# The order of the matmuls in a GEMM chunk of a decoder layer: output tile by output tile, or k tile, product, output tile

## The reference

```python
h = rmsnorm(x, norm_mix)
parts = split(h @ w_in)                      # u, Bg, Cg, q/k/v of 3 head groups, g_a, g_b
A = (Bg * dwconv3(Cg * u)) @ w_conv_out      # short gated convolution
B = merged_attention(q, k, v) @ w_attn_out   # 3 dilated window groups; the samples read caches
x = x + (sigmoid(g_a) * A + sigmoid(g_b) * B) @ w_out
up, gate = split(rmsnorm(x, norm_ffn) @ w_ffn_in)
x = x + (silu(dwconv3(gate) + b) * up) @ w_ffn_down
y = rmsnorm(x, norm_final)
```

## Time and profile before

| | |
|---|---|
| median of 3 runs | 1557.56 us (1556.78 to 1562.81) |
| the profiled execution: span, first to last instruction | 1559.4 us |
| TensorE matmuls (PE) | busy 1527.8 us, 98%, 12354 matmuls |
| TensorE weight loads (PEld) | busy 1512.0 us, 97% |
| VectorE (DVE) | busy 895.9 us, 57% |
| ScalarE (ACT) | busy 693.6 us, 44% |
| GpSimd (POOL) | busy 75.8 us, 5% |
| mean granted TensorE clock | 0.993 |
| HBM | 210 GB/s over the span |

### The profile page before, as it was taken

How to read it: one execution, slowest core, us unless ns; L and a number is a source line. 1 busy time by engine, 2 the same in 40 slices (tenths; PEclk the granted TensorE clock), 3 DMA queues, 4 the chain that set the end, 5 groups by cost and what they waited for, 6 DMA issues and landing times.

```text
span 1559.4 us, 32031 instructions
## 1 busy us (share of the span) xinstructions
PE 1527.8 (98%) x12354; PEld 1512.0 (97%) x12354; DVE 895.9 (57%) x1057; ACT 693.6 (44%) x761; POOL 75.8 (5%) x145
## 2 busy tenths in 40 slices
PE   8999999999989999999999999989999999999997
PEld 8999999999988889999999999989999999999997
DVE  8646455756655434676665555664444656556554
ACT  7444444434444334444554444443333444444452
POOL 2000001002130000010000000000000000000000
PEclk9999999999999999999999999999999999999998
DMA  8867576557986636555577777775555666565552
GB/s 276 276 179 250 178 228 184 150 150 200 258 246 198 215 112 201 175 162 188 176 243 243 230 232 222 244 240 163 178 183 176 169 188 183 173 184 183 184 176 97
DMA packets 145141, 307.79 MB, mean 197 GB/s; under 512 B 10145, under 2 KB 10273, under 8 KB 144561
## 3 DMA queue, kind: packets, MB, share of 16 engines
q1 hardware_dynamic: 139120, 268.73, 56.2%
q0 software_dynamic: 5952, 38.12, 7.6%
HBM read 301.39 MB, written 26.38 MB: 210 GB/s over the span
## 4 chain that ended last, share of the span: by engine, by line
PE 96%; DVE 2%; issue 1%; ACT 0%; DMA 0%; SPq 0%; DVEq 0%; ACTq 0%
PE acc L919 31%; PE acc L920 31%; PE acc L921 31%; PE side L1058 1%; DVE w_lo L554 1%; PE side L1012 1%; PE side L991 1%; DMA raw<-w_in 0%; ACT w_hi L356 0%; DVE yg L900 0%; PE side L1003 0%; DVE tf L809 0%; PE side L978 0%; DVE tf L813 0%; DVE gate_a L731 0%
## 5 line engine op out<-in xcount | busy, mean ns | idle before, releaser
L554 DVE TENSOR_TENSOR w_lo<-raw,w_hi 128x1024 fp32r<-128x1024 f32 x503 | 617.2, 1236 | 546.5 <-ACT w_hi L356 544.4
L356 ACT ACTIVATE w_hi<-raw 128x1024 fp32r<-128x1024 f32 x503 | 530.0, 1059 | 742.1 <-PE acc L921 680.8
L919 PE MATMUL acc<-h_hi,w_hi 128*128 128x264 f32 x2872 | 821.5, 286 | 6.6 <-DVE gate_a L731 4.6
L921 PE MATMUL acc<-h_hi,w_lo 128*128 128x264 f32 x2872 | 817.5, 285 | 0.2 <-issue 0.2
L920 PE MATMUL acc<-h_lo,w_hi 128*128 128x264 f32 x2872 | 817.6, 285 | 0.0
L919 PEld LDWEIGHTS acc<-h_hi,w_hi 128*128 128x128 f32 x2872 | 542.8, 189 | 9.1 <-DVE gate_a L731 5.2
L920 PEld LDWEIGHTS acc<-h_lo,w_hi 128*128 128x128 f32 x2872 | 541.9, 189 | 0.1
L921 PEld LDWEIGHTS acc<-h_hi,w_lo 128*128 128x128 f32 x2872 | 540.7, 188 | 0.4 <-issue 0.4
L919 PE MATMUL acc<-f_hi,w_hi 128*128 128x264 f32 x704 | 201.1, 286 | 4.0 <-DVE f_lo L871 4.0
L921 PE MATMUL acc<-f_hi,w_lo 128*128 128x264 f32 x704 | 200.8, 285 | 1.2 <-issue 1.2
L920 PE MATMUL acc<-f_lo,w_hi 128*128 128x264 f32 x704 | 200.8, 285 | 0.0
(11 more groups left out here) (188 smaller groups left out, 851.6 us busy)
## 6 DMA issues: line engine op xcount, KB each, us to landing
raw<-w_in SPq DMA_DIRECT2D x183, 512.0 KB, 4.2
raw<-w_ffn_in SPq DMA_DIRECT2D x176, 512.0 KB, 4.1
raw<-w_ffn_down SPq DMA_DIRECT2D x88, 512.0 KB, 4.2
raw<-w_out SPq DMA_DIRECT2D x32, 512.0 KB, 4.5
s_kv<-cache POOLq DMA_DIRECT2D x16, 1020.0 KB, 9.1
raw<-w_conv_out SPq DMA_DIRECT2D x16, 512.0 KB, 4.6
raw<-w_attn_out SPq DMA_DIRECT2D x8, 512.0 KB, 4.7
s_kv<-cache POOLq DMA_DIRECT2D x8, 508.0 KB, 5.0
```

Of the source, the lines that this page charges most:

```text
L356: act.activation(w_hi[:, s % RING], raw[:, s % RING], ACT.Copy).then_inc(hi_ready, 1)
L554: dve.tensor_tensor(w_lo[:, s % RING], raw[:, s % RING], w_hi[:, s % RING].bitcast(F32), ALU.subtract).then_inc(lo_ready, 1)
L919: pe.matmul(out, w_hi[:, slot, k, cols], m_hi[:, kt + k, :], start=first and k == 0, stop=False)
L921: mm = pe.matmul(out, w_lo[:, slot, k, cols], m_hi[:, kt + k, :], start=False, stop=last and k == 1)
```

## The change

In every chunk that is not its group's last, the matmuls are written k tile by k tile, in it product by product, and in it output tile by output tile. Each matmul then writes another bank than the one before it. The waits on `psum_free` stand ahead of the first four matmuls of a group, one for each bank. A group's last chunk keeps its order, tile by tile, and its `tile_done`. `first_chunk` is not touched.

```diff
                 pe.wait_ge(lo_ready, 4 * quad + s + 1)
                 slot = s % RING
+                if not last:
+                    for k in range(2):
+                        for n, (w, x_k) in enumerate(((w_hi, m_hi), (w_hi, m_lo), (w_lo, m_hi))):
+                            for m in range(TILES):
+                                if first and k + n == 0:
+                                    pe.wait_ge(psum_free, TILES * group + m + 1)
+                                mm = pe.matmul(acc[:, m, 0:T], w[:, slot, k, m * P:(m + 1) * P], x_k[:, kt + k, :],
+                                               start=first and k + n == 0, stop=False)
+                    mm.then_inc(slots_free, 1)
+                    return
                 for m in range(TILES):
                     if first:
                         pe.wait_ge(psum_free, TILES * group + m + 1)
```

## The result

| | before | changed |
|---|---|---|
| median of 4 runs each | 1559.28 us | 1578.70 us (1578.05 to 1582.83) |
| ratio | | 1.0129, 95% interval 1.0110 to 1.0149 |
| profiled execution: time, span | span 1559.4 us | time 1579.13 us, span 1577.3 us |
| mean granted clock | 0.993 | 0.996 |

The change makes the kernel slower by 1.3%, 20 us (17 to 23). Forecast were 1583 us and a range of 1568 to 1600.

The account below looks back on a forecast made before the run. TensorE was taken to bound the kernel (96% of the chain). Pauses of 23.3 + 0.3 + 2.0 = 25.6 us on the 1559.4 us span gave 1585.0, stated as 1583 because the span lies 1.8 us above the median; range 1568 to 1600.

Parts of the forecast that it names:

- the ordinary and the partly covered boundaries: Between groups: 49 ordinary boundaries pause TensorE for 23.3 us in all; two partly covered ones cost 0.3 us.
- attn_out: Stage with late bank reads: new order loses 1.0 us at each of three boundaries, not in full; 2.0 us taken.
- (a): In 437 chunks, 10,488 steps on TensorE go to another bank than the one before; cost taken as 0.
- The spare 1 ns per step: Uncertainty of the steps that change bank: 1 ns either way not excluded, 10 us each way, kept for the range.
- (b): Group's first chunk: bank waits move to matmuls 1 to 4; TensorE pauses for last read's end + 0.05 − 0.25 us.
- the three types: Boundaries by reader of the banks: FFN type pauses 0.44 us, L818 type 0.56 us, ScalarE type 0.39 us.
- Restarting adds nothing: After a wait at a boundary, the held matmul runs 0.1 us behind its load, as undisturbed; no extra cost.
- The ring: In attn_out, t_hi, w_hi, w_lo and reads turn by themselves in 7.1 us without TensorE, so the loss can't add up fully.
- gate_a, 0: Four boundaries after gate_a groups: pauses disappear in the key-load loop, cost 0; uncovered, 0.5 to 1.0 us each.
- Faster and slower steps: Rivals on TensorE's step: 10 ns less, 105 us gained, 1478, chance 0.12; 3 ns more, +31 us, 1614, chance 0.08.
- Absorption: Rival: boundary pauses shrink TensorE's other waits, above all in gate_a; 10 to 15 us back, 1568 to 1573; chance 0.10.
- The falling clock: Rival: each boundary's pause drops TensorE to 1.2 GHz for one chunk; 132 us, 1715; chance 0.03.

Follow-up runs that it names:

- second measurement: The changed kernel once more, on one chip with the kernel before: 1577.21 us, ratio 1.0150 (1.0127 to 1.0172).
- the middle chunks alone: New order only in chunks neither first nor last in their group, against the kernel before: 1556.57 us against 1555.11, ratio 1.0010.
- the pairs: New order in middle chunks; in a group's first chunk banks 0 and 1 alternate, then 2 and 3; against the kernel before: 1555.47 us, ratio 0.9993.
- the split's place: VectorE's weight split moved to between bank reads 2 and 3: in the kernel before 1555.25 us, ratio 1.0000; in the changed kernel 1609.57 us, ratio 1.0347.
- the late split: The changed kernel with VectorE's weight split moved from between reads 0 and 1 to between reads 2 and 3: 1609.57 us, ratio 1.0347.
- the run with gate_a alone: New order only in the four gate_a groups, all their chunks but the last, against the kernel before: 1555.96 us against 1555.46, ratio 1.0005.
- the run with all chunks: The changed kernel with each group's last chunk in the new order too: 1712.01 us, ratio 1.1004 (1.0973 to 1.1034).

## Why the prediction was right

The direction, the mechanism and the size hold. Point by point:

- *The sum.* 25.6 us were forecast against 20 us (17 to 23) and, in the second measurement, 23 us (20 to 27) measured: the sum lies above the first interval and within the second. The pauses themselves came as summed: the ordinary and the partly covered boundaries, priced at 23.3 + 0.3 us, lost 23.5 and 23.6 in two profiles, attn_out 1.1 instead of 2.0. That makes 24.6 or 24.7. The two profiled spans differ by only 17.9 us; the kernel before lost about 5 us to its clock in gate_a and conv_out and 1.3 us to a wait in down_b in its execution. Why the medians of the first measurement lie 20 us apart and not 25 isn't shown. That the forecast of 1583 us lies only 4 us from the median is due in part to the kernel before, which ran 1.7 us above the 1557.56 that it started from.
- *(a), alternating steps, taken as 0.* Shown by the middle chunks alone (1.0010) and by the pairs (0.9993). That one step in six already turned to another bank in the old order, at no other pace, was enough evidence. The spare 1 ns per step wasn't needed: the step moved by less than 0.1 ns, about 1 us in all.
- *(b), the pause per boundary.* This is also where the rule of the Trainium skill on rotating banks ("Perfetto Trace Analysis", Matmuls) pointed, and the split's place shows it: with the waits apart a read of 1.4 us is overlapped, with the waits together it is paid. 0.44, 0.56 and 0.39 us predicted, 0.46, 0.56 and 0.39 measured in the three types. The rule used (end of the last read + 0.05 us − 0.25 us) also gave the 1.2 us of the late split and its 31 us in total, measured as 31 to 34.
- *Restarting adds nothing.* Held: after the late load at 940.62 the next starts at 940.73.
- *attn_out, 2.0 us (1.3 to 3.1).* Too large, though the reason given for absorption was right. The stage grew by 1.5 us (25.3 to 26.8), but 0.5 of that is the ordinary pause behind gate_b's last group. Its own boundaries lost 0.5, 0.6, 0.0 and, into w_out, 0.0 us, the same in both profiles of the changed kernel: 1.1 us. At the last two TensorE had already waited 1.2 us for the late reads in the old order, ahead of a first chunk's seventh matmul, and at the one before them 0.6 us; now it waits 1.2 us in all at each of the three, from the second matmul on (one of them before, then two changed):

```profile
666.22 0.39 PE L919 MATMUL acc<-att_hi,w_hi 128*128 128x264 f32 x1 [0.95 <-DVE tf L809]
```

```profile
663.08 1.07 PE L919 MATMUL acc<-att_hi,w_hi 128*128 128x264 f32 x3 [0.52 <-DVE tf L809]
670.15 1.07 PE L919 MATMUL acc<-att_hi,w_hi 128*128 128x264 f32 x3 [0.52 <-DVE tf L809]
```

  The ring turns in 670.15 − 663.08 = 7.07 us, as before (7.1), so at its pace a pause inside it adds nothing. The earlier trace rows shows such a wait too, ahead of 673.28.
- *gate_a, 0.* The run with gate_a alone is in keeping (+0.8 us, −1.6 to +3.1), but can't tell 0 from 2.7. Nor can the lengths of the two stages, clock taken off: some 1.4 us may have been paid there. Open.
- *The rivals.* Faster and slower steps: not there. Absorption: only where the prediction had it. The falling clock: not with pauses of 0.4 to 0.6 us (granted clock 0.996), but real at many of the pauses of 2.2 us. Its price of 132 us supposed a whole chunk at half speed at every boundary; in the run with all chunks it came to about 43 us.
- *A count was wrong:* 504 chunks, not 503 (the first is split in halves). It changes no term.

## What to carry to other kernels

An accumulating loop that visits its output tiles in turn asks for all its PSUM banks at once; one that finishes a tile before the next asks for them one after another. If the next group reuses the banks of the last, write down for each bank when the reader lets go and when the first matmul asks: only that difference is paid, once per group, and at both ends, since tiles that end together are also read late. Here the step didn't depend on the order of banks at all, so the tile-by-tile order costs nothing in the middle and saves 1.3 to 1.5% at the seams; where banks shall alternate for another reason, alternate in pairs in the first chunk.

## What the runs showed of the hardware

- A step of fp32r matmuls with a weight load each (128 × 128) is 112 ns at 128 and at 232 columns, 118 at 256, 121 at 264: trimming columns gains nothing below some 240 (an estimate: 118 ns less 0.4 ns for each of the 15 columns below 256 is the floor).
- Pauses of about 2.2 us at each group start, single matmuls among them, went with a clock at half speed behind 10 of the 12 group starts of ffn_a, and behind 1 of the 10 of ffn_b; pauses of 1.2 us in the run with the late split left the mean clock at 0.996.
- With 128 columns in the middle chunks, the clock stayed at 0.50 from 13 to 45 us though TensorE is shown busy all the time; with 232 it was at 1.00. It is one execution of each, and the cause stays open.
- From the end of VectorE's read of a bank to the start of the weight load that waited for it passed 0.05 to 0.06 us (940.57 to 940.62, 958.42 to 958.48), and the loads behind followed as usual.
